# Down stage of a two-block transformer on one core: VectorE reads activation and gates from SBUF, and ScalarE's copy of the gates into PSUM goes

## What is computed

```python
top_sc, pos = lax.top_k(cand, PEER_TOPK)
gate = jax.nn.softmax(top_sc, axis=-1)              # 8 heads x 16 experts for each token
act = jax.nn.gelu(jnp.einsum('thkd,td->thk', u_tab[eb], hb), approximate=False)
return jnp.einsum('thk,thkd->td', gb * act, v_tab[eb])
```

## Time and profile before

| | us |
|---|---|
| median of 3 runs | 3418.14 |
| lowest and highest | 3417.44, 3432.96 |
| the profiled execution, device time | 3415.01 |
| its span, first to last instruction | 3413.2 |

### The profile page before, as it was taken

One profiled execution on the slowest core, in us unless ns is written; L12 is line 12 of the kernel. 1 busy time (PEld: TensorE's weight loads), 2 busy tenths in 40 slices (PEclk: granted clock), 3 DMA queues, 4 the chain that ended last, 5 costly groups with the idle time before them and its releaser, 6 DMA issues.

```text
span 3413.2 us, 46478 instructions
## 1 busy us (share of the span) xinstructions
PE 3213.3 (94%) x16195; PEld 2774.4 (81%) x16195; DVE 2236.4 (66%) x4113; ACT 1360.5 (40%) x1999; POOL 1723.1 (50%) x922
## 2 busy tenths in 40 slices
PE   6999999989999999979999999898999999899998
PEld 4787787779999999979999998756888886478886
DVE  5787898769968677646666645286854332857553
ACT  4555432333454544434444443365322223632221
POOL 2222343434767667657787754662444443034443
PEclk8999999999999999989999999999999999999999
DMA  5434422223689797999999953211222232122222
GB/s 208 156 119 162 150 93 80 93 86 112 209 294 333 249 338 247 325 346 337 343 350 356 335 181 108 85 54 48 94 98 99 95 107 102 48 68 99 98 94 87
DMA packets 190046, 587.55 MB, mean 172 GB/s; under 512 B 19585, under 2 KB 52737, under 8 KB 189601
## 3 DMA queue, kind: packets, MB, share of 16 engines
q1 hardware_dynamic: 83936, 303.08, 25.5%
q10 hardware_dynamic: 69092, 148.25, 12.0%
q0 software_dynamic: 36864, 134.23, 11.8%
HBM read 532.92 MB, written 67.24 MB: 176 GB/s over the span
## 4 chain that ended last, share of the span: by engine, by line
PE 66%; DVE 13%; DMA 8%; issue 5%; ACT 3%; POOL 3%; ACTq 0%; DVEq 0%; SPq 0%; POOLq 0%
PE ps L417 19%; PE ps L419 19%; PE ps L418 19%; DMA ring<-panels 6%; POOL ring_r L2201 3%; PE ps L653 2%; DMA arena<-u_rows,arena 2%; PE ps L781 2%; DVE ps L1781 1%; PE ps L516 1%; ACT high_w L894 1%; PE ps L770 1%; DMA arena<-v_rows,arena 1%; DVE arena L1849 1%; DVE arena L1846 1%
## 5 line engine op out<-in xcount | busy, mean ns | idle before, releaser
L2201 POOL TENSOR_TENSOR ring_r<-ring,high_w 128x1024 fp32r<-128x1024 f32 x552 | 1365.6, 2476 | 1446.1 <-ACT high_w L894 1443.9
L417 PE MATMUL ps<-uT_r,high_w 128*128 128x512 f32 (+1 forms) x2608 | 986.2, 378 | 17.1 <-POOL ring_r L2201 11.5
L419 PE MATMUL ps<-uT_r,ring_r 128*128 128x512 f32 (+1 forms) x2608 | 963.6, 369 | 0.0
L894 ACT ACTIVATE high_w<-ring 128x1024 fp32r<-128x1024 f32 x552 | 582.2, 1057 | 888.1 <-PE ps L419 645.6
L418 PE MATMUL ps<-sq_r,high_w 128*128 128x512 f32 (+1 forms) x2032 | 737.3, 363 | 0.0
L418 PE MATMUL ps<-part,high_w 128*128 128x384 f32 (+1 forms) x1840 | 664.2, 361 | 0.0
L417 PE MATMUL ps<-part,high_w 128*128 128x384 f32 (+1 forms) x1664 | 599.9, 361 | 35.8 <-POOL ring_r L2201 17.3
L419 PE MATMUL ps<-part,ring_r 128*128 128x384 f32 (+1 forms) x1664 | 595.4, 358 | 0.0
L417 PEld LDWEIGHTS ps<-uT_r,high_w 128*128 128x128 f32 x2608 | 493.6, 189 | 89.3 <-POOL ring_r L2201 14.4
L419 PEld LDWEIGHTS ps<-uT_r,ring_r 128*128 128x128 f32 x2608 | 492.7, 189 | 63.4
L418 PEld LDWEIGHTS ps<-sq_r,high_w 128*128 128x128 f32 x2032 | 384.1, 189 | 39.1 <-issue 1.0
(11 more groups left out here) (354 smaller groups left out, 4065.9 us busy)
## 6 DMA issues: line engine op xcount, KB each, us to landing
ring<-panels SPq DMA_DIRECT2D x568, 512.0 KB, 3.4
gdram<-arena ACTq DMA_DIRECT2D x48, 512.0 KB, 7.3
arena<-adram ACTq DMA_DIRECT2D x128, 192.0 KB, 4.8
arena<-gdram ACTq DMA_DIRECT2D x14, 1536.0 KB, 16.8
adram<-arena ACTq DMA_DIRECT2D x102, 192.0 KB, 5.2
arena<-ada_rest ACTq DMA_DIRECT2D x32, 512.0 KB, 4.6
strips_dram<-btab ACTq DMA_DIRECT2D x4, 3584.0 KB
arena<-strips_dram ACTq DMA_DIRECT2D x24, 448.0 KB, 3.4
```

Of the source, the lines that this page charges most:

```text
L417: t_.matmul(out, wh, xh[:, 0:n], start=(k == 0), stop=False)
L419: last = t_.matmul(out, wl, xh[:, 0:n], start=False, stop=(k == KT - 1))
L894: s_.activation(high_w[:, j % RING], ring[:, j % RING], ACT.Copy).then_inc(hi_ready, 1)
L2201: g_.tensor_tensor(ring_r[:, j], ring[:, j], high_w[:, j], ALU.subtract).then_inc(lo_ready, 1)
```

## The change

`gate_copy` goes, with its semaphore. `gated_act` reads the gates from `gi` itself, so both its inputs now lie in SBUF, and only its output is the PSUM bank. The waits that `gate_copy` made move to `gated_act`: on the load of `gi`, on the bank (`hid_ready`, an event of VectorE's own), and for the first odd tile on the last reading of bank 7. The wait ahead of the next load of `gi` is now on `gated_ps`.

```diff
@@ ScalarE
-            def gate_copy(m):
-                g, k = m // 8, m % 8
-                if k == 0:
-                    act.wait_ge(g_in[g % 2], 16 * (g // 2 + 1))
-                if m >= 2:
-                    act.wait_ge(hid_ready[0], m - 1)
-                s_.activation(ps[:, chain_bank(m), 0:DENSE].rearrange("p (a t) -> p a t", t=64), gi[:, g % 2, :, 64 * k:64 * k + 64],
-                              ACT.Copy).then_inc(gate_ps, 1)
...
-                if n == 8 * GROUPS - 2:
-                    act.wait_ge(hot_ready, 5 * 32 * DENSE_TILES)
-                    for m in range(2):
-                        gate_copy(m)
...
                 fetch(m + 4)
-                gate_copy(m + 2)
...
                 if s % 8 == 0 and s // 8 + 2 < GROUPS:
-                    act.wait_ge(gate_ps, s + 8)
+                    act.wait_ge(gated_ps, s + 8)
                     gates(s // 8 + 2)
-                if m + 2 < 8 * GROUPS:
-                    gate_copy(m + 2)
@@ VectorE
             def gated_act(m):
-                ve.wait_ge(gate_ps, m + 1)
+                if m % 8 == 0:
+                    ve.wait_ge(g_in[m // 8 % 2], 16 * (m // 16 + 1))
+                if m == 1:
+                    ve.wait_ge(g_evac, 32 * DENSE_TILES + 1)
+                if m >= 2:
+                    ve.wait_ge(hid_ready[0], m - 1)
                 ve.wait_ge(a_in[m % 4], 16 * (m // 4 + 1))
                 chain = ps[:, chain_bank(m), 0:DENSE]
-                v_.tensor_tensor(chain, act_in[:, m % 4, :], chain, ALU.mult).then_inc(gated_ps, 1)
+                v_.tensor_tensor(chain.rearrange("p (a t) -> p a t", t=64), act_in[:, m % 4, :].rearrange("p (a t) -> p a t", t=64),
+                                 gi[:, m // 8 % 2, :, 64 * (m % 8):64 * (m % 8) + 64], ALU.mult).then_inc(gated_ps, 1)
```

More of the change, by code:

```diff
@@ L311, in build @@
         u_done, v_done = sem("u_done"), sem("v_done")
-        gate_ps, gated_ps, hid_high = sem("gate_ps"), sem("gated_ps"), sem("hid_high")
+        gated_ps, hid_high = sem("gated_ps"), sem("hid_high")
         a_in = [sem(f"a_in{i}") for i in range(4)]
```

## The result

The kernel after takes 3422.8 us in the median of 20 runs, the one before 3415.4 us in 20 runs on the same chips. The ratio is 1.0025, with a 95% interval of 1.0016 to 1.0035: about 8.5 us slower (5.5 to 12), which is within 0.5%. A second set of runs of the unchanged kernel after gave 1.0031 (1.0015 to 1.0048). One of e1's 12 timed runs took 6315 us, far from its other eleven (3407 to 3423 us), and is left out of its ratio. The profiled execution took 3417.44 us, its span is 3415.6.

The account below looks back on a forecast made before the run. TensorE was taken as the bound, with at most 15 us idle in the middle. Terms -3.2 + 2 + 3.2 = +2 us made 3415.0 into 3417, 3420 for the median; range 3411 to 3443 us.

Parts of the forecast that it names:

- sum of +2 us: Whole kernel: -3.2 for the copies, +2 for GpSimd held, +3.2 for the start, making 3415.0 into 3417 us.
- -4 to +11 us: Bounds of the main case for the whole kernel's change in time, given 0.62, counted as same.
- The copies' going, -3.2 us: Middle of the stage: without the gate copy's wait for `hid_rest`, TensorE's six stalls go, -3.2 us.
- my six stalls: TensorE waits in the middle where the panel had landed but ScalarE stood in the gate copy, together 3.2 us.
- `gated_act` held by the port: Product with two SBUF inputs blocked until GpSimd's subtraction ends, 87 of 128 times; VectorE loses 77 us, counted as covered.
- that rival: Port does not bite because the product's output is in PSUM: -4 us, 3414 us; chance 0.10.
- The start, +3.2 us: Start of the stage: tile 2's product comes behind two back-to-back subtractions, 3.2 us later, and TensorE waits for it.
- the row of 5.07 us: Earlier trace row: a product begun at 1302.14 came behind two more subtractions; used to choose +3.2 over +0.9 us.
- GpSimd held, +2 us: Subtractions begun under `gated_act` lose at most 0.55 us each; 0 to 8 us over 15 stalls, a quarter taken.
- Tiles are made eight panels ahead …: VectorE to TensorE: VectorE's 77 us are covered by 134 us of waits and the tiles' lead, so 0 us.
- The lock: Loop of subtraction, `gated_act`, `hid_top`, rounding: 4.40 us a panel against 4.15, 27 us slower, 3447; chance 0.15.
- VectorE as the bound: Waits for gathered rows stay at 107 us, slots of 4.6 us against 4.37; 3448, up to 3470 us; chance 0.10.

Follow-up runs that it names:

- e1: Kernel after, but the product's second input is its own PSUM bank and the gates are left out; ratio to before 0.9989.
- e3: Kernel before with the gate copy behind the weight panel's rounding on ScalarE; ratio to before 0.9987.
- r4: e3 run again, gate copy behind the rounding; ratio to before 0.9985.
- e8: e3 with the product for panel s+1 ahead of `residual(s)` on VectorE; ratio to before 0.9982.
- r1: Kernel after, run and profiled again without any edit; ratio to before 1.0031.
- r2: Kernel before, run and profiled again without any edit; ratio to before 0.9999.
- e6: e1 with two more VectorE operations, PSUM to PSUM, on the halves of the tile; ratio to before 1.0003.
- e5: Kernel after with one wait added on ScalarE, for `hid_rest(s+8)` ahead of the rounding; ratio to before 0.9988.
- e2: Kernel before with the product reading two SBUF inputs, the copies and their waits kept; ratio to before 1.0004.
- e4: Kernel after with `hid_top` and `fetch` behind the rounding on ScalarE; ratio to before 1.0048.
- r3: e5 run again, the wait for `hid_rest` added ahead of the rounding; ratio to before 1.0002.
- e7: Kernel after with the product for panel s+1 ahead of `residual(s)` on VectorE; ratio to before 1.0001.

## Why the prediction was right in its result, and which step was wrong

The time (3420 predicted, 3422.8 measured, no difference by 0.5%) came out, and the sum of +2 us was too small by about 6.5. That 8.5 us lies within my -4 to +11 is partly luck: 8 of the 11 stood for stalls through a held GpSimd, which did not come, and the loss came from a term that I had put at nothing. Point by point:

- **The copies' going, -3.2 us.** Not contradicted, not shown: e1, e3 and r4 gained 4 to 5 us by their ratios, with intervals of 4 to 6 us to either side. Two of my six stalls, the ones of 0.25 us, were not the copy's: they come one panel behind a longer stall, and came again (0.24 to 0.27 us) in e1, e3, r4 and e8.
- **`gated_act` held by the port.** Right, in size too. VectorE lost 94 us over the 128 products (87 in r1) where I had 77, and a held product ends 0.42 us after the subtraction, as interpolated from the earlier trace rows. That the output is a PSUM bank makes no difference, so that rival falls.
- **The start, +3.2 us.** Right: +3.3 in all seven profiles with two SBUF inputs. The choice between the Trainium skill's sentence in "SBUF — State Buffer", section "Who interferes with whom", that whoever issues first has the pair for the whole instruction while the other fully blocks (+0.9 us by my reading of it), and the row of 5.07 us was rightly made for the row: the product at 1489.27 came behind both subtractions. Whether tile 0 came the 0.8 us earlier can't be read: TensorE's stop ahead of it is 9.9 and 11.2 us in before and r2, 11.3 and 8.3 in after and r1.
- **GpSimd held, +2 us.** Not seen as a wait of TensorE: its waits for the subtraction fell, to 6.5 and 10.8 us. With those for `hid_rest` they make 16.8 and 18.1 us, above the 12 to 16 that I had said the changed profile would show.
- **"Tiles are made eight panels ahead … on the path to TensorE I therefore count nothing."** This is the step that failed. The eight panels hold for a group's first tile; the eighth is made in the slot ahead of the panel that needs it, with a margin of 0.9 to 4.9 us. I compared sums (134 us of waits against 77) where the margin at 15 places decides. It cost 8.8 us of waits and 2.4 us of lowered clock, took over a part of the subtraction's waits (-5.0 in all), and made of my -3.2 + 2 = -1.2 us for the middle the +6.6 measured.
- **The lock.** The loop is real, with just the 4.40 us a panel (4.44 in the rows above, 4.40 for the subtraction behind them), and for no longer than five slots in a row. I had its price wrong in place: I let it act by a late subtraction against TensorE's 4.15 us, while it acts sooner, by a late eighth tile. What ends it I gave as the late landings, and the traces say otherwise: all 16 runs end where ScalarE issues a `gates` load, ahead of the late landings that come with this load.
- **VectorE as the bound.** Fell: the waits for gathered rows went down to 50 us, and e6 carries the same load.

I had also called the copy's wait a pure cost. e5 shows that it had a use once the product has two SBUF inputs: it spaced the subtraction from the product.

## What to carry to other kernels

Ask for every tile not how far ahead the first of its group is made but when the last is due, and hold a new delay against that margin at each boundary, not against an engine's idle sum. Where VectorE and GpSimd stream side by side, keep one input of VectorE's operation in PSUM where you can: here the copy of 0.50 us a tile on an engine with time to spare was cheaper than the port. And before a wait goes, ask which order it enforced; the better edit here was to keep the copy and move it behind the rounding (e3, r4, e8: 0.9982 to 0.9987, with intervals that end at or just below 1).

## What the runs showed of the hardware

- A VectorE operation with two SBUF inputs can stay blocked through two GpSimd instructions that follow each other at once. At tile 2 it came behind both subtractions in all seven profiles with such a product (3.64 to 4.02 us). It is no rule: ten other products of these profiles (tiles 115 to 119), begun in the first of two such subtractions, ended 0.4 us behind the first. A gather's issue and a subtraction can do the same, here in the kernel after:

```profile
1912.15 3.44 DVE L1938 TENSOR_TENSOR ps<-arena 128x384 f32<-128x384 f32 x1
...
1911.78 0.95 POOL L2289 DMA_INDIRECT arena<-v_rows,arena  x1 [0.16 <-issue]
1912.75 2.41 POOL L2190 TENSOR_TENSOR ring_r<-ring,high_w 128x1024 fp32r<-128x1024 f32 x1
```

The product began during the gather and ended 0.43 us after the subtraction. Seven more products did so (2.93 to 3.45 us), but 22 others that began in such a gather's issue took 0.55 to 0.57 us and were not held. I had not counted gathers here.

- The issue of one of this stage's gathers takes 1.09 us in the median in each of the seven profiles with two SBUF inputs (up to 1.25 in the kernel after), and 0.95 us in the other seven.
- A single wait can lower TensorE's granted clock for some 3.6 us. It did so after waits of 1.73 to 3.13 us in 13 places of the middles (two in after, one in r1, two in e2, one in e4, one in r3, one in e6, four in e7, one in e8), and did not after others of 2.24 us (after) and 2.31 us (r3). What sets them apart I did not find.
